# Delta rule: the rows of cumulated decays go through DRAM and a broadcast load, in place of a product with ones

## The reference, cut to what matters

```python
def gated_delta_rule_chunked(q, k, v, g, beta):
    ...
    gc = jnp.cumsum(g.reshape(b, h, n, CHUNK), axis=-1)
    ...
    diff = gc[..., :, None] - gc[..., None, :]
    decay = jnp.where(incl, jnp.exp(jnp.where(incl, diff, 0.0)), 0.0)
    kb = k * beta
    m = jnp.where(strict, jnp.einsum("bhnid,bhnjd->bhnij", kb, k) * decay, 0.0)
    ...
    qk = jnp.where(incl, jnp.einsum("bhnid,bhnjd->bhnij", q, k) * decay, 0.0)
    q_dec = q * jnp.exp(gc)[..., None]
```

## Time and profile before

| | us |
|---|---|
| median of 3 executions | 2973.35 (2973.16 to 2974.43) |
| the profiled execution | 2974.32 |
| its span in the trace | 2972.4 |
| PE busy | 2939.4 (99% of the span) |
| DVE busy | 2002.0 (67%) |
| ACT busy | 1426.6 (48%) |
| POOL busy | 310.2 (10%) |

### The profile page before, as it was taken

The page is one execution under the profiler, slowest core; times in us unless marked ns, Lnnn a source line. Parts: engine busy times, 40 slices in busy tenths (PEclk is TensorE's granted clock), DMA queues, the critical chain, the costliest instruction groups (busy, mean ns, idle before and its releaser), DMA issues.

```text
span 2972.4 us, 44233 instructions
## 1 busy us (share of the span) xinstructions
PE 2939.4 (99%) x15407; PEld 2413.6 (81%) x15407; DVE 2002.0 (67%) x2620; ACT 1426.6 (48%) x1870; POOL 310.2 (10%) x265
## 2 busy tenths in 40 slices
PE   8999999999999999999999999999999999999998
PEld 6888877788888888887888877777888888888887
DVE  5765777656667777667678677777655666666666
ACT  6445556544444444445555443334545444444444
POOL 0001960000000000000000154442000000000000
PEclk9999999999999999999999999999999999999999
DMA  6555454456555555554565533333765555565554
GB/s 216 180 185 176 136 170 133 152 200 206 185 186 189 179 188 193 192 188 142 189 219 183 175 116 123 122 121 122 239 220 192 189 191 187 187 191 189 188 190 147
DMA packets 145147, 525.80 MB, mean 177 GB/s; under 512 B 16416, under 2 KB 17184, under 8 KB 144160
## 3 DMA queue, kind: packets, MB, share of 16 engines
q1 hardware_dynamic: 139760, 503.72, 51.4%
q0 software_dynamic: 1536, 11.78, 1.0%
q10 hardware_dynamic: 3760, 9.05, 1.0%
HBM read 516.09 MB, written 8.39 MB: 176 GB/s over the span
## 4 chain that ended last, share of the span: by engine, by line
PE 95%; DVE 2%; issue 1%; ACT 1%; DMA 0%; POOL 0%; ACTq 0%; DVEq 0%; POOLq 0%; SPq 0%
PE bank L2168 57%; PE bank L2173 28%; PE bank L2265 1%; PE bank L2589 1%; PE bank L2196 1%; DVE w_lo L1366 1%; ACT w_hi L757 1%; PE bank L2336 1%; PE bank L2618 0%; PE bank L2406 0%; PE bank L2500 0%; PE bank L2273 0%; DMA w_raw<-weights 0%; PE bank L2351 0%; PE bank L2815 0%
## 5 line engine op out<-in xcount | busy, mean ns | idle before, releaser
L1366 DVE TENSOR_TENSOR w_lo<-w_raw,w_hi 128x1024 fp32r<-128x1024 f32 x952 | 1194.2, 1264 | 787.5 <-ACT w_hi L757 786.5
L757 ACT CAST w_hi<-w_raw 128x1024 fp32r<-128x1024 f32 x952 | 1000.3, 1052 | 1387.9 <-PE bank L2173 1361.5
L2168 PE MATMUL bank<-w_hi,a_hi 128*128 128x512 f32 x2784 | 1110.2, 399 | 4.8 <-ACT w_hi L757 2.9
L2168 PE MATMUL bank<-w_hi,a_lo 128*128 128x512 f32 x2784 | 1088.0, 391 | 0.0
L2173 PE MATMUL bank<-w_lo,a_hi 128*128 128x512 f32 x2784 | 750.7, 390 | 0.0
L2168 PEld LDWEIGHTS bank<-w_hi,a_hi 128*128 128x128 f32 x2784 | 524.3, 188 | 121.6 <-issue 10.8
L2173 PEld LDWEIGHTS bank<-w_lo,a_hi 128*128 128x128 f32 x2784 | 523.5, 188 | 110.6
L2168 PEld LDWEIGHTS bank<-w_hi,a_lo 128*128 128x128 f32 x2784 | 524.7, 188 | 105.1 <-issue 1.9
L2168 PE MATMUL bank<-w_hi,m_lo 128*128 128x512 f32 x480 | 186.7, 389 | 0.0
L2168 PE MATMUL bank<-w_hi,m_hi 128*128 128x512 f32 x480 | 186.7, 389 | 0.0
L1438 DVE TENSOR_TENSOR h<-h,bank 128x512 f32<-128x512 f32 x232 | 148.5, 681 | 19.9 <-PE bank L2173 19.9
(11 more groups left out here) (411 smaller groups left out, 2512.9 us busy)
## 6 DMA issues: line engine op xcount, KB each, us to landing
w_raw<-weights SPq DMA_DIRECT2D x952, 512.0 KB, 3.9
gate<-gate_st ACTq DMA_DIRECT2D x8, 512.0 KB, 3.9
h<-gate ACTq DMA_DIRECT2D x8, 512.0 KB, 5.2
gain<-gains POOLq DMA_DIRECT2D x3, 1024.0 KB, 7.2
h<-x_tok SPq DMA_DIRECT2D x4, 512.0 KB, 10.8
w_proj_sb<-w_proj POOLq DMA_DIRECT2D x1, 2048.0 KB, 9.9
h_rest<-h POOLq DMA_DIRECT2D x1, 2048.0 KB, 9.0
h<-h_rest POOLq DMA_DIRECT2D x1, 2048.0 KB, 10.4
```

The lines of the kernel that those rows point to most:

```text
L757: nc.scalar.copy(w_hi[:, s, :], w_raw[:, s, :]).then_inc(hi_ready, 1)
L1366: V.tensor_tensor(w_lo[:, s, :], w_raw[:, s, :], w_hi[:, s, :].bitcast(F32), ALU.subtract).then_inc(lo_ready, 1)
L2168: T.matmul(psum[t][:], left[:, t * P:(t + 1) * P], wh, start=start and j == 0 and n == 0, stop=False)
```

## The change

The row of gc is no longer made by a product. Once, ahead of the loop, PE turns the whole of gc (128 tokens x 32 columns) into 32 rows (`sums_turned`), ACT copies them to SBUF (`gc_T`, in a part of sp2 that is free) and stores them with four DMAs to a DRAM tensor `gc_rows`, one row of 512 values for each head. POOL then loads the row of each head onto all 128 partitions of `hd.gs`: for the first turn before the loop, for the next one in the middle of each turn. DVE and ACT read `hd.gs` in place of `hd.bank[0]`. Since `hd.gs` now has to live until the second set of differences, the masked m (L1961) goes to `hd.r`. POOL's loop has three turns, and the fourth is written out behind it, without loads.

```diff
+        gc_rows = nc.dram_tensor("gc_rows", (DNH, TT * 2 * P), F32, kind="Internal").ap()
...
+        gc_T = sp2[0:TT * 2 * DNH, 0:4].rearrange("p m n -> p (m n)")
...
-            with pool.Fori(0, DNH // 2) as i:
+            def rows_of_heads(i):
+                for hd in heads:
+                    pool.dma_start(flat(hd.gs), gc_rows[bass.ds(2 * i + hd.x, 1), :].to_broadcast([P, TT * 2 * P])).then_inc(dn_rows, 16)
+
+            def turn(i, last=False):
...
-                for hd in heads:
-                    nc.gpsimd.tensor_tensor(hd.gs, cums, of_head(g2, hd.x), ALU.mult).then_inc(dn_rows, 1)
...
                             nc.gpsimd.tensor_tensor(hd.eT, hd.eT, cums, ALU.mult).then_inc(dn_eTm, 1)
+                            if hd.x == 1 and not last:
+                                pool.wait_ge(dn_egb, heads[1].of(i))
+                                rows_of_heads(i + 1)
...
+            pool.wait_ge(rows_stored, 4 * 16)
+            rows_of_heads(0)
+            with pool.Fori(0, DNH // 2 - 1) as i:
+                turn(i)
+            turn(DNH // 2 - 1, last=True)
...
             split(Q_MIX, 0, 1)
+            act.wait_ge(narrow_mm, 3)
+            nc.scalar.copy(gc_T, bank[0][0:TT * 2 * DNH, 0:P]).then_inc(narrow_copied, 1)
             qkT_evac(0)
+            act.wait_ge(narrow_copied, 3)
+            for t in range(TT):
+                for d in range(2):
+                    r = (t * 2 + d) * DNH
+                    act.dma_start(gc_rows[:, (t * 2 + d) * P:(t * 2 + d + 1) * P], gc_T[r:r + DNH]).then_inc(rows_stored, 16)
             qkT_evac(2)
...
-                    nc.scalar.activation(flat(hd.qd), hd.bank[0][:], ACT.Exp).then_inc(dn_egb, 1)
+                    nc.scalar.activation(flat(hd.qd), flat(hd.gs), ACT.Exp).then_inc(dn_egb, 1)
...
-                        last = V.tensor_scalar(dst[:, t, d], hd.units(0)[:, t, d], col(gc, t, d, hd), 0.0, ALU.subtract, bound)
+                        last = V.tensor_scalar(dst[:, t, d], hd.gs[:, t, d], col(gc, t, d, hd), 0.0, ALU.subtract, bound)
...
+                dve.wait_ge(dn_rows, 2 * 16 * (i + 1))
                 for hd in heads:
-                    dve.wait_ge(dn_gcb, hd.of(i))
                     differences(hd, hd.eN, ALU.max)
...
+            def sums_turned():
+
+                pe.wait_ge(dn_pre, 1)
+                pe.wait_ge(pair_free[0], 2 * (U_MIX + 1))
+                T.transpose(bank[0][0:TT * 2 * DNH, 0:P], gc[:].rearrange("p t d a -> p (t d a)"), ident[:]).then_inc(narrow_mm, 1)
+                qk_turned(0, 1)
...
-                        if k == 1:
-                            pe.wait_ge(dn_egb, hd.of(i))
...
-                    pe.wait_ge(dn_rows, hd.of(i))
-                    T.matmul(hd.bank[0][:], ones[:], flat(hd.gs), start=True, stop=True).then_inc(dn_gcb, 1)
-                for hd in heads:
                     pe.wait_ge(dn_qk, hd.of(i))
                     pe.wait_ge(dn_free, hd.of(i))
```

More of the change, by code:

```diff
@@ L474, in program @@
         z2_scaled, fr_ready = sem("z2_scaled"), sem("fr_ready")
-        (dn_free, dn_qk, dn_rows, dn_in, dn_gcb, dn_kk, dn_diff, dn_eT, dn_eN, dn_egb, dn_eTm, dn_qd, dn_m, dn_mk,
+        (dn_free, dn_qk, dn_rows, dn_in, dn_kk, dn_diff, dn_eT, dn_eN, dn_egb, dn_eTm, dn_qd, dn_m, dn_mk,
          dn_t, dn_rT, dn_r0, dn_r, dn_z, dn_zz, dn_rz, dn_tz, dn_uw, dn_u, dn_wT, dn_qkm, dn_ws, dn_vn, dn_so, dn_s) = (
             sem("dn_" + n) for n in (
-                "free", "qk", "rows", "in", "gcb", "kk", "diff", "eT", "eN", "egb", "eTm", "qd", "m", "mk", "t", "rT",
+                "free", "qk", "rows", "in", "kk", "diff", "eT", "eN", "egb", "eTm", "qd", "m", "mk", "t", "rT",
                 "r0", "r", "z", "zz", "rz", "tz", "uw", "u", "wT", "qkm", "ws", "vn", "so", "s"))
@@ L483, in program @@
             "f_mm", "f_half_ready", "f_out", "f_odd_ready", "f_summed", "fr_hi_ready", "fr_lo_ready"))
-        mix_ready = sem("mix_ready")
+        mix_ready, rows_stored = sem("mix_ready"), sem("rows_stored")
         out_scaled, stored = sem("out_scaled"), sem("stored")
@@ L1960, in _ @@
                     dve.wait_ge(dn_m, hd.of(i))
-                    step(V.tensor_tensor(hd.gs, hd.m, level[:, 0].unsqueeze(1).to_broadcast([P, TT, 2, P]), ALU.mult))
+                    step(V.tensor_tensor(hd.r, hd.m, level[:, 0].unsqueeze(1).to_broadcast([P, TT, 2, P]), ALU.mult))
                     V.tensor_tensor(hd.t.rearrange("p t d s -> p (t d) s"), ident[:].unsqueeze(1).to_broadcast([P, 2 * TT, P]),
-                                    hd.gs.rearrange("p t d s -> p (t d) s"), ALU.subtract).then_inc(dn_t, 1)
+                                    hd.r.rearrange("p t d s -> p (t d) s"), ALU.subtract).then_inc(dn_t, 1)
                 split(q + 1, 0, 1)
@@ L2566, in qk_turned @@
                     last.then_inc(dn_qkT, 1)
+            def sums_turned():
[3 more added lines that the diff above has]
+                qk_turned(0, 1)
             chunk(Q_Z2 + 2, 1, U_Z2, a_hi, a_lo,
-                  between={4: lambda: qk_turned(0, 1), 5: lambda: qk_turned(2, 3), 6: lambda: qk_turned(4, 5), 7: lambda: qk_turned(6, 7)})
+                  between={4: sums_turned, 5: lambda: qk_turned(2, 3), 6: lambda: qk_turned(4, 5), 7: lambda: qk_turned(6, 7)})
             steps = SEQ // CHUNK
@@ L2574, in _ @@
             pe.wait_ge(dn_qkT_evac1, 4)
+            pe.wait_ge(narrow_copied, 3)
             with pe.Fori(0, DNH // 2) as i:
```

## The result

The changed kernel takes **2983.25 us** (median of 9 runs, 2977.68 to 2985.5); the kernel before, run beside it, 2973.68 (9 runs, 2973.16 to 2975.08). That is 9.6 us more; the ratio, taken over all runs and not from the two medians, is 1.0029, with a 95% interval of 1.002 to 1.0037. The prediction said 2972.6, with a range up to 2977.0. The profiled execution of after took 2983.44, its span is 2981.8.

A forecast was written before the change was run, and what follows sets the result against it. PE was taken as the bound, busy 77.47 of 78.9 us a turn. Terms -0.3 - 0.6 + 0.15 = -0.75 us against the median 2973.35 gave 2972.6; own range 2971.0 to 2974.0, 8 in 10 range 2970.8 to 2977.0.

The forecast's parts named there:

- Step 1: Three boundaries between turns: without the product with ones, PE idles waiting for DVE's output additions; gain 0.1 us each, 0.3 in all.
- Step 2: First turn: head 1's k and q products start 0.9 us earlier, DVE waits for the loaded rows; net gain 0.6 us.
- Step 3: Making the rows ahead of the loop: one PE transpose costs 0.15 us; ACT's copy and stores cost nothing.
- Step 4: Inside three turns: POOL's two load issues, 1.08 us, delay its k=2 mask within 0.6 us cover; w_lo pair change taken as 0.
- clock rival: At turn starts, PE's idle time and small products drop the granted clock, 1.5 us a fall, 2974.1 to 2978.6; chance 0.30.
- POOL late: Inside turns: POOL's two issues stretch to 2.0 us and PE waits for POOL's mask, 2973.6 to 2976.9; chance 0.10.
- saving: At turn starts: bank[1] is free in time, so all 8.1 us of products with ones go, 2964.1; chance 0.04.
- late rows: Each turn: loads go out only at the turn's end, so landing and issues show four times, 9 us, 2982; chance 0.04.

## Why the prediction was wrong

**Step 1 was right.** The product was the cover of a wait for DVE: idle 1.93 us at all three boundaries, released by the output additions. Kept or not, the product made little difference (2973.58 and 2975.5), and the two runs with another order on DVE show the rest of that step's reading.

**Step 2 came out with the wrong sign**, though its first half was right in kind. The first slab of the first turn starts at 1740.32 instead of 1741.84, so 1.5 us earlier; I had 0.9, since POOL's copies took 1.17 us together and not the 2.23 that I took from the earlier trace rows. They had taken 2.23 where DVE's w_lo ran beside them; here it begins at 1739.53, when they are nearly done. But DVE was held by the rows until 1742.45, where I had 1741.1:

```profile
1739.15 1.23 PE L2696 MATMUL bank<-delta 128*64 128x64 f32 x32 [1.89 <-POOL delta L707]
...
1742.45 0.68 DVE L1917 TENSOR_SCALAR delta<-delta,gc 128x128 f32<-128x128 f32 x3 [1.70 <-DMA delta<-gc_rows]
...
L1917 DVE TENSOR_SCALAR delta<-delta,gc x64: 268/273/286, 1742.4 to 1996.8; 128x128 f32<-128x128 f32 x64
```

These are of after: PE and DVE in the first turn, then a single line, ns at least, median, at most. A subtraction takes 273 ns. The issues began 0.36 us later than I had them, and these two loads took 4.1 and 4.4 us to land and not 3.6, which is the median of all eight. So DVE's matrix t, which I had followed for head 1 alone, comes late for both heads: head 1's products on it start at 1751.27 instead of 1750.62. The net gain of 0.6 was a loss of 0.65. The fall at the turn's start hides the wait, because it slows PE. In the kernel with the loads at the end, whose clock held there, PE stands idle for it:

```profile
1748.09 0.66 PE L2702 MATMUL bank<-ident_sb,delta 128*128 128x128 f32 x4 [1.30 <-DVE delta L1979]
```

So most of what the earlier start of PE gave would have gone without the fall too.

**Step 3 was right**: one transpose, and neither the copy nor the stores on ACT's queue held anything up. The copy took 0.25 us and the four stores 1.57, and the w_hi behind them starts at 1730.10 instead of 1730.05.

**Step 4 failed, and with it the sum.** The mask product for k=2 was never late, which was the question I had put to it. The term that failed is the w_lo pair, which I took at 0 "nearest to the row of that very place", with the slowest pair of the trace, 5.70 us, as its upper bound. The pairs were 6.02, 4.49, 7.30 and 4.49. In the first and third turn PE waited 2.13 and 3.42 us instead of 0.6 and 0.7: 4.2 us more, and behind the long wait the clock fell once more. The bound of 1.1 a turn came from a trace in whose loop POOL issues no DMA. The experiments show that just this is what changes the pair: two issues of 512 bytes do it (2989.25), 512 KB from ACT's queue don't (2972.85), nor does the same shift by copies (2971.86). A row of an operation beside other neighbours was no bound for it.

**The clock rival was the right mechanism with too small a chance.** I gave one fall the time 2974.1 and four 2978.6. There were four in the profiled execution, three after waits at a turn's start and one behind the wait of step 4, so some 6 us: three of 1.7, and in the first turn the part of it that was not a wait for t anyway. Its odds of 0.30 were set too low: the earlier trace rows had shown both patterns, idle time and small products, and the change puts the one behind the other. The rule of the Trainium skill that the prediction quoted (TensorE: Matmul & The Clock Gate, section What's actually happening: activity releases the throttle) went the right way, and the trace agrees: 0.50 after 1.93 us of idle time and light products. But falls alone don't explain the result. Without the DMA issues in the middle, with the same idle time at the boundaries, the profile had one fall in the loop and the time was 2975.5, within the range. (The range's upper end, two falls and the POOL case, adds up to 3.0 + 1.0 over the forecast, 2976.6 and not 2977.0; it makes no difference here.)

**POOL late, the saving, and late rows** did not come. "POOL late" had POOL as the victim and DVE as the one in the way; it was the other way round. The two issues took 1.11 us in the middle of the turn and 1.14 at its end, and were never stretched to 2.0. The Trainium skill (SBUF — State Buffer, section SBUF: two separate sides) warns of descriptors that POOL cannot write while DVE holds the ports; no run here shows that case.

Left open: why an issue makes POOL keep DVE off over several instructions, in eight of the ten long pairs to the end of its run and in the two of some 6 us not quite; whether idle time or distance ends it; and why a pair that arrives 0.10 us behind a change of POOL's instruction gets its turn after all wherever that happens (4.49 us, with the issues or without). The turns of the changed kernel differ by that.

## What to carry to other kernels

A DMA issue on POOL is not just its half microsecond. Issued ahead of an unbroken run of POOL's work it can shut DVE's operations with two inputs in SBUF (w_lo here) out for several of POOL's instructions, mostly until that run ends. In this kernel it did no harm where POOL stood idle behind it, and none from ACT's queue; put it where POOL stands idle afterwards, or on another engine's queue. When taking work from the bounding engine, look for the wait that the work covered, and shorten that in the same edit: here the one gave nothing, the other nothing, and both together 6 us. Of a wait on a shared resource a row with other neighbours gives no upper bound.

## What I had not expected of the hardware

- Behind two DMA issues of 512 bytes each on POOL, two w_lo of DVE (2.4 us alone) took 8.04 us, while POOL's products ran at their full speed (1.0 to 1.3 us each). With copies in the place of the issues, and with the same arrival, the pair took 3.4 to 4.1 us and POOL's products stretched instead, two of them from 2.5 to between 3.5 and 4.5 us.
- A copy of 512 columns on POOL takes 0.60 us where the products of the same size take 1.02 to 1.27.
- The granted clock fell to 0.50 after 1.9 us of idle time followed by 64-column products at some boundaries (1822 and 1986) and not at another of the same shape (1902), and after an idle time of 3.42 us in the middle of a turn. With 0.56 us of idle time ahead of the same products no fall was seen at the three boundaries of each of two kernels.
